# A two-layer hybrid decoder step: index scores earlier, two feature tiles moved into the attention loop, probabilities scaled on ScalarE

## What is computed

```python
(q, k, v, qi, ki, wi, bx, gb, gc, glu, zg, xbc, dt) = jnp.split(u @ p['w_in'], cuts, axis=-1)
# indexer: 8 heads x 32, one shared key; every query keeps its best 128 keys
s = jnp.einsum('bqhd,bsd->bqhs', qi, ki) * IDX_DIM ** -0.5
score = jnp.einsum('bqhs,bqh->bqs', jax.nn.relu(s), wi * N_IDX_HEADS ** -0.5)
_, idx = lax.top_k(where(causal, score, -inf), topk)
# 4 heads x 64 over the kept keys
logits = einsum(q, k[idx]) * HEAD_DIM ** -0.5;  p = softmax(logits);  y = einsum(p, v[idx])
```

## Time and profile before

| | us |
|---|---|
| three runs | 1465.22, 1466.51, 1470.06 (median 1466.51) |
| the profiled execution: its own time | 1465.05 |
| its span | 1463.3 |
| PE busy | 1368.9 (94%) |
| DVE busy | 1017.8 (70%) |
| ACT busy | 652.4 (45%) |
| POOL busy | 184.2 (13%) |

### The profile page before, as it was taken

One profiled execution on the slowest core, in us unless ns is written; L12 is line 12 of the kernel. 1 busy time (PEld: TensorE's weight loads), 2 busy tenths in 40 slices (PEclk: granted clock), 3 DMA queues, 4 the chain that ended last, 5 costly groups with the idle time before them and its releaser, 6 DMA issues.

```text
span 1463.3 us, 29326 instructions
## 1 busy us (share of the span) xinstructions
PE 1368.9 (94%) x11014; PEld 1267.0 (87%) x11014; DVE 1017.8 (70%) x2141; ACT 652.4 (45%) x1202; POOL 184.2 (13%) x132
## 2 busy tenths in 40 slices
PE   5999979997999999999879998899979999999997
PEld 5789865787999999999767997648979999999996
DVE  5489898744899999322366898987259999982223
ACT  4443335444556666322244422445344665653222
POOL 0334312021000000001030442121100000000000
PEclk9999989998999999999979999999989999999998
DMA  7443231221523333433254333212223233335321
GB/s 267 123 126 101 66 94 61 93 72 44 159 73 108 107 101 101 155 91 98 95 165 127 100 84 94 66 69 82 88 81 108 88 114 102 100 97 160 88 88 59
DMA packets 223892, 149.85 MB, mean 102 GB/s; under 512 B 13650, under 2 KB 218810, under 8 KB 222758
## 3 DMA queue, kind: packets, MB, share of 16 engines
q1 hardware_dynamic: 221174, 141.09, 32.4%
q0 software_dynamic: 2624, 7.48, 1.4%
HBM read 128.92 MB, written 16.03 MB: 99 GB/s over the span
## 4 chain that ended last, share of the span: by engine, by line
PE 80%; DVE 14%; ACT 3%; issue 2%; SPq 1%; DMA 0%; POOL 0%; DVEq 0%; ACTq 0%
PE PS L684 29%; PE PS L1149 24%; PE PS L785 11%; PE PS L756 2%; PE PS L757 2%; PE PS L758 2%; PE PS L912 1%; DVE side L2016 1%; DVE x L2281 1%; PE PS L663 1%; PE PS L700 1%; PE PS L739 1%; PE PS L740 1%; PE PS L741 1%; DVE arena L1768 1%
## 5 line engine op out<-in xcount | busy, mean ns | idle before, releaser
L1149 PE MATMUL PS<-b_hi,a_hi 128*128 128x260 f32 x1008 | 286.2, 284 | 3.0 <-DVE last_lo L2364 2.2
L1149 PE MATMUL PS<-b_lo,a_hi 128*128 128x260 f32 x1008 | 284.4, 282 | 0.0
L2169 DVE TENSOR_TENSOR w_lo<-ring,w_hi 128x640 fp32r<-128x640 f32 (+2 forms) x88 | 87.5, 995 | 242.4 <-ACT w_hi L1403 242.1
L1149 PEld LDWEIGHTS PS<-b_hi,a_hi 128*128 128x128 f32 x1008 | 189.9, 188 | 4.5 <-DVE last_lo L2364 2.7
L1149 PEld LDWEIGHTS PS<-b_lo,a_hi 128*128 128x128 f32 x1008 | 190.3, 189 | 0.0
L1403 ACT CAST w_hi<-ring 128x1024 fp32r<-128x1024 f32 (+2 forms) x92 | 80.1, 871 | 234.3 <-PE PS L684 234.3
L785 PE MATMUL PS<-u_hi,w_hi 128*128 128x260 f32 x576 | 123.4, 296 | 13.6 <-ACT hid L1345 13.6
L684 PE MATMUL PS<-hid_hi,w_lo 128*128 128x260 f32 x656 | 132.3, 283 | 0.0
L684 PE MATMUL PS<-hid_hi,w_hi 128*128 128x260 f32 x656 | 132.1, 283 | 0.0
L684 PE MATMUL PS<-hid_lo,w_hi 128*128 128x260 f32 x656 | 131.9, 283 | 0.0
L1149 PE MATMUL PS<-b_hi,s_lo 128*128 128x260 f32 x432 | 122.1, 283 | 0.0
(11 more groups left out here) (401 smaller groups left out, 3329.1 us busy)
## 6 DMA issues: line engine op xcount, KB each, us to landing
ring<-in_ffn_gate SPq DMA_DIRECT2D x44, 512.0 KB, 3.7
ring<-in_ffn_up SPq DMA_DIRECT2D x44, 512.0 KB, 3.7
ring<-in_w_in SPq DMA_DIRECT2D x36, 512.0 KB, 3.6
ring<-in_ffn_down SPq DMA_DIRECT2D x32, 384.0 KB, 3.4
ring<-in_ffn_down SPq DMA_DIRECT2D x32, 320.0 KB, 3.0
x_store<-x SPq DMA_DIRECT2D x4, 2080.0 KB
x<-x_store SPq DMA_DIRECT2D x4, 2080.0 KB, 8.3
ring<-in_w_out SPq DMA_DIRECT2D x16, 512.0 KB, 4.2
```

The costliest lines, as they stand in the source:

```text
L1149: ins = pe.matmul(bank(ACC[up][to])[:, 0:HALF], w[:, k, :], b[:, k, :], start=(start and k == 0 and w is whi and b is bhi), stop=(k == KC ...
L2169: dve.tensor_tensor(w_lo[part % 2][:, 0:n, :], raw[part % 4][:, 0:n, :], w_hi[part % 2][:, 0:n, :].bitcast(F32), ALU.subtract).then_inc(pa ...
```

## The change

1. The low parts of slabs 1 and 2 are made by DVE right after the normalisation, not by POOL. ACT casts all three pieces of slabs 1 and 2 ahead of the token tiles.
2. The order of the token tiles is a list: four tiles of slab 0, then (1, 0), and only then the samples of slab 0. The transposition of the index queries stands within that tile, after its second k. The 24 index products stand three at each of eight places, at the quarters of tiles (1, 1) and (1, 2), the first three after the samples' tile.
3. The addition of the `dt` bias on DVE moves behind the rotation of q, and the rotation of k and of the samples behind the eighth round of top-k.
4. `SPREAD_FROM` goes from 7 to 5 and with it `LOOP_TILES` from 11 to 9: tiles 9 and 10 move into the loop, whose portions grow from 246 products to 336.
5. DVE's multiplication by the inverted denominator (L2120) goes; ACT writes the scaled copy, at the start of its step.

```diff
-        SPREAD_FROM = 7
+        SPREAD_FROM = 5
-        STEP_PRODUCTS = (14, 12, 13, 9, 13, 9, 13, 9, 13, 9, 9)
+        STEP_PRODUCTS = (18, 16, 17, 13, 17, 14, 17, 14, 17, 13, 12)
         LOOP_TILES = SPREAD_FROM + NS * PER_SPREAD // PER_TILE
-        IDX_PLACES = [(1, 1, 1), (1, 2, 0), (1, 2, 1), (1, 3, 0), (1, 3, 1), (1, 4, 0)]
-        IDX_AT = {place: range(4 * i, 4 * i + 4) for i, place in enumerate(IDX_PLACES)}
+        TOK_TILES = [(0, t) for t in range(QT)] + [(1, 0), (0, QT)] + [(1, t) for t in range(1, QT + 1)] +             [(2, t) for t in range(QT + 1)]
+        TURN_QI = (0, QT, 0)
+        IDX_PLACES = [(0, QT, 3)] + [(1, 1, q) for q in range(4)] + [(1, 2, q) for q in range(3)]
+        IDX_AT = {place: range(3 * i, 3 * i + 3) for i, place in enumerate(IDX_PLACES)}
...
+                            if k % 2:
+                                if (s, t, k // 2) == TURN_QI:
+                                    pe.wait_ge(*past(layer, rope_done, 2))
+                                    pe.wait_ge(*past(layer, tok_ready, QT))
+                                    turn(tok_qi, 0, bank(4))
+                                    turn(tok_qi, 1, bank(5))
+                                    turn(ki_four, 0, bank(6))
+                                idx_products((s, t, k // 2))
...
-                    slab_upper(1, 0)
+                    for s in range(1, N_TOK):
+                        for i in range(len(tok_pieces[s])):
+                            slab_upper(s, i)
...
+                        if 1 <= j <= len(STEPS):
+                            i = j - 1
+                            keys = (STEPS[i][0] + 1) * P
+                            act.wait_ge(*past(layer, denom_turned, i + 2))
+                            act.activation(rect[:, i % 2, 0:keys], rect[:, i % 2, 0:keys], ACT.Copy, scale=rden[:, i % 2:i % 2 + 1])\
+                               .then_inc(prob_ready, 1)
                         if j < len(STEPS):
...
+                    for s in range(1, N_TOK):
+                        for i in range(len(tok_pieces[s])):
+                            slab_lower(s, i)
                     dve.memset(tap_col[96:P], 0.0).then_inc(tap_cols_ready, 1)
...
                     for r in range(TOPK_PROMPT // 8):
-                        if r == 4:
+                        if r == 8:
                             rope_tiles(tok_k, HEADS, HD, 16, tab, 2 * (QT + 1) + QT).then_inc(rope_done, 1)
...
                             dve.wait_ge(*past(layer, exp_done, i + 1))
-                            step(dve.reciprocal(rden[:, b2], denom[:, b2]))
-                            settle()
-                            dve.tensor_scalar(rect[:, i % 2, 0:keys], rect[:, i % 2, 0:keys], rden[:, b2], None, ALU.mult)\
-                               .then_inc(prob_ready, 1)
+                            dve.reciprocal(rden[:, b2], denom[:, b2]).then_inc(denom_turned, 1)
...
                     for f in range(2, len(feat_tiles)):
                         tile_lower(f)
-                        if f == 6:
+                        if f == SPREAD_FROM:
```

More of the change, by code:

```diff
@@ L386, in hybrid_decoder @@
                                                        sem("mixed_out", 4))
+        denom_turned = x8_turned
+        per_layer[denom_turned.num] = 16
         vec, conv_c_done = sem("vec"), sem("conv_c_done", 2)
@@ L728, in _ @@
                               .then_inc(states_turned, 1)
[L729 to L753, removed]
-                                u_k, lo_k = u_hi[:, k, t * P:t * P + m], m_lo[k][:, t * P:t * P + m]
-                                hi, lo = tok_k_of(tw_hi, s, k), tok_k_of(tw_lo, s, k)
-                                pe.matmul(to, u_k, hi, start=(k == 0), stop=False)
-                                pe.matmul(to, u_k, lo, start=False, stop=False)
-                                last = pe.matmul(to, lo_k, hi, start=False, stop=(k == KC - 1))
-                                if k == KC // 2 - 1:
-                                    idx_products((s, t, 0))
-                            last.then_inc(tok_summed, 1)
-                            g += 1
-                            if s == 1 and t == 0:
-                                pe.wait_ge(*past(layer, rope_done, 2))
-                                pe.wait_ge(*past(layer, tok_ready, QT + 1))
-                                turn(tok_qi, 0, bank(4))
-                                turn(tok_qi, 1, bank(5))
-                                turn(ki_four, 0, bank(6))
-                            idx_products((s, t, 1))
@@ new lines, in _ @@
+                        m = P if t < QT else NS
+                        to = bank(tok_bank(g))[0:m, 0:tok_w[s]]
+                        pe.wait_ge(*past(layer, tok_ready, g - 1 if g > QT + 1 else g - QT + 1))
+                        for k in range(KC):
+                            if t == 0 and k in [a for a, _, _, _ in tok_pieces[s]]:
+                                pe.wait_ge(*past(layer, slab_lo, sum(len(p) for p in tok_pieces[:s]) +
+                                           [a for a, _, _, _ in tok_pieces[s]].index(k) + 1))
+                            u_k, lo_k = u_hi[:, k, t * P:t * P + m], m_lo[k][:, t * P:t * P + m]
+                            hi, lo = tok_k_of(tw_hi, s, k), tok_k_of(tw_lo, s, k)
+                            pe.matmul(to, u_k, hi, start=(k == 0), stop=False)
+                            pe.matmul(to, u_k, lo, start=False, stop=False)
+                            last = pe.matmul(to, lo_k, hi, start=False, stop=(k == KC - 1))
+                            if k == KC - 1:
+                                last.then_inc(tok_summed, 1)
+                            if k % 2:
[6 more added lines that the diff above has]
+                                idx_products((s, t, k // 2))
```

110 lines of the change are left out of this document (55 added, 55 removed).

## The result

The changed kernel took 1472.76 us in the median of ten runs (1471.34 to 1474.81), the kernel before 1466.53 in ten. The ratio is 1.0040, with an interval from 1.0031 to 1.0050: slower by 0.4%, where 0.6% faster was forecast, and outside the range. The profiled execution took 1474.61 us, 1.9 above its median.

A forecast was written before the change was run, and what follows sets the result against it. PE was taken to bound the kernel ahead of the loop, DVE in it until the moved products make PE last. Per layer −10.6 + 6.5 = −4.1, −8.2 for two: 1458 us, 0.6% faster, range 1446 to 1471.

The forecast's parts named there:

- Ahead of the loop: Before the attention loop, PE bounds and DVE keeps up; two tiles leave, 10.6 us gained a layer.
- +0.9 for the stretch before the feature tiles: Token products ahead of the feature tiles: −0.6 idle wait, +0.5 interruptions by index products, +1.0 PE held for additions.
- a wait of PE for DVE's additions: Ahead of the loop, denser index products wait for DVE's score additions: between nothing and 2.5 us, taken as 1.0.
- PE's own work in the loop: Loop up to step 11: 336 products, 40.4 us, and the rest make PE busy for 56.5 us.
- The clock: Loop to step 11: the 3.3 us lost at granted clock 0.50 go, since PE is denser now.
- Rival C: In the loop the clock falls all the same; 3.3 to 4.7 us return a layer, 1465 to 1468; chance 0.21.
- The waits: PE's waits for tile copy-outs in the loop: five instead of three, 8.5 to 11.3 us; step 11 +6.5.
- rival D: In the loop, copy-outs come late behind ACT's scaled copy and exponential; slower from a mean wait of 3.2, 1474; chance 0.14.
- The late steps: Steps 11 to 15: PE is nearly always busy, DVE's savings count nothing, the rest follows as before; priced at 0.
- DVE's side: Loop steps 0 to 10: division goes, −3.0 us; POOL subtractions add up to 4.4; DVE takes 58.3 to 62.7.

The follow-up runs named there:

- aligned: The changed kernel with 16 products in each half step of the loop instead of 12 to 18; 1455.0 us, 0.9910 of the kernel before.
- one_long_wait: aligned with 15, 15 and 14 products in the half steps of steps 8, 9 and 10, moving one tile end into step 9; 1467.8 us.
- before_aligned: The kernel before with 12 products in each half step of steps 0 to 9 and none in step 10; 1467.7 us, ratio 0.9999.
- div_on_dve: The changed kernel with the division of the probabilities back as DVE's multiplication, without ACT's scaled copy; 1481.9 us, 1.0094 of the kernel before.

## Why the prediction was wrong

- **Ahead of the loop: right.** −11.5 + 0.9 = −10.6 was forecast, −10.1 came. DVE kept up: the first rotation is undisturbed, as the changed kernel's timeline shows, and of its waits for copy-outs of tokens one of 2.0 us is left. The +0.9 for the stretch before the feature tiles (+1.0 measured) is right in the sum by luck, not in its terms: the idle time of 0.62 went, as I had it, but the rest came as 1.6 us more busy time; a wait of PE for DVE's additions, which I had priced at 1.0, does not show.

```profile
43.63 0.42 DVE L1767 TENSOR_TENSOR arena<-arena,cst 128x256 f32<-128x256 f32 x1 [1.06 <-ACT arena L1306]
```

- **PE's own work in the loop: right in kind and size.** 56.5 us at full clock were forecast, and aligned has 56.3. PE became the bound, and its waits for probabilities went (none to step 11).
- **The clock: the first step that failed.** "My sum drops these 3.3 us, since PE is denser now." They stayed: 60.2 us busy where 56.5 were forecast, +3.7 a layer. PE is denser in the mean, but the clock was at its lower level behind the waits of 2.85 and 3.69 us, and one_long_wait shows with a single edit that one wait grown to 4.41 brings that level back. Rival C had this at 0.21, with "3.3 to 4.7 return". The page that I weighed for the other side (the Trainium skill, TensorE: Matmul & The Clock Gate, section "What's actually happening") says that the throttled state is the default and that activity releases it; this loop agrees on the side of C, with a mean granted clock of 0.93 where two waits are that long and 1.00 in aligned, where none is over 1.69. The longest wait alone does not decide it: before_aligned lost the clock behind 1.79, and the kernel before kept it through 2.98.
- **The waits: the second.** The mean of the earlier trace rows, 2.27, would have been right: 2.32 was measured. I took less (9.9 us for five in place of 11.6), with the argument that a late PE finds ACT waiting. ACT did wait in three of five, 1.69 each. But the third (2.85) stood behind a scaled copy and an exponential, and the fifth (3.69) in the one step that has table loads ahead of the copy-out; I had not laid the new tile ends against ACT's order step by step. That is the mechanism of rival D in two places rather than in four; by its own measure, a mean of 3.2, D did not happen.
- **The late steps: the third, not in the sum at all.** I held that what DVE saves there counts nothing, and did not ask what PE would wait for there. +2.3 us in layer 0 and +2.5 in layer 1 came. It is idle time: PE is busy for 34.00 us instead of 33.87, at a granted clock of 0.91 instead of 0.90, but its waits are 3.5 us instead of 1.2. PE waits three times there for a scaled copy that stands behind reciprocals and, once, behind ACT's table load and six decay exponentials; the kernel before has one wait of 0.9 us for the multiplication there and one of 0.3 for a DMA. Waits of PE in the late steps, changed kernel and kernel before, and timeline of ACT, the scaled copy behind the longest wait of the changed one:

```profile
PE PS L960 <- ACT arena L1417: 3.5, 3, 1.8
```

```profile
PE PS L965 <- DVE arena L2120: 0.9, 1, 0.9
PE PS L886 <- DVEq L2085: 0.3, 1, 0.3
```

```profile
242.92 0.61 ACT L1417 ACTIVATE arena<-arena,small 128x384 f32<-128x384 f32 x1 [4.36 <-DVE small L2119]
```

So the failed term is PE's waits behind step 11, priced at nothing and measured at +2.3. Whether the scaled copy makes them stays open: the one of 1.85 stands behind DVE's reciprocal, for which ACT had waited 4.36 us, and div_on_dve, without any scaled copy, still has a wait of 3.3 us for DVE's multiplication there and a late stretch of 39.8.

- **Sum**, in terms of a layer: forecast −4.1; clock +3.7, waits +1.7, late steps +2.3 and ahead of the loop +0.5 make +4.1, and +4.3 was measured.
- **DVE's side** was right for its part: its first five steps together took 1.9 us less than before (1.5 in layer 1), and POOL's subtraction still doubles a DVE piece (2.32 to 4.47), but none of it bound.

## What to carry to other kernels

When work is moved into another engine's gap, the gap is not the idle time, but what is left of it after the waits that the moved work brings along: list each place where the moved work needs something back (here a PSUM bank), and lay it against the order of the engine that gives it back, step by step, above all where that engine has rare long pieces (table loads). Cut such work so that its ends fall where the bounding engine has something else to do; here the same 336 products in equal portions are worth 17.8 us. Where a wait of PE grows, look at the granted clock behind it: 2.7 us more of wait cost 4.5 to 5.4 on the way to step 11 here, though not every long wait did so. And before a few us are read out of one trace, look at how far the executions of one kernel lie apart, and at which of them was traced.

## What the runs showed of the hardware

- One wait of PE of 4.41 us in place of 1.69 in each layer cost 4.5 to 5.4 us on the way to step 11, 1.4 to 2.4 of them as products at the lower clock. The medians of the two programs differ by 12.8 us, of which the traces don't place all.
- In six kernels in which no wait of PE on that way was over 1.7 us, the granted clock there was 1.00 in both layers; in the other eleven, whose longest waits there were 2.3 to 4.7 us, it was 0.89 to 0.98. The longest wait does not decide it alone: before_aligned fell to 0.50 behind a wait of 1.79 us (its one of 2.63 came later), and the kernel before stayed at 1.00 around one of 2.98. What else decides was not tried.
- DVE is held by a POOL subtraction even where its own instruction is tiny. The kernel before, timeline of DVE in layer 0's loop, the multiplication that usually takes 0.29 us, and POOL's subtraction that began 0.01 us later:

```profile
191.74 2.45 DVE L2120 TENSOR_SCALAR arena<-arena,small 128x128 f32<-128x128 f32 x1
```

```profile
191.75 2.36 POOL L2524 TENSOR_TENSOR w_lo<-ring,w_hi 128x1024 fp32r<-128x1024 f32 x1 [11.21 <-ACT w_hi L1291]
```

A multiplication on the path can thus cost eight times its price, by where POOL's work happens to fall. The changed kernel's 32 scaled copies on ACT took 0.40 to 0.72 us, for widths of 128 to 512, four of them beside a POOL subtraction, and none took over 0.02 us more than another of its width.
